# A fp32 two-layer decoder trunk on one NeuronCore: large tiles moved to multiples of 512 bytes, the router's matmul turned round, and result-free matmuls in its waits

## What is computed (the reference, cut)

```
for layer in range(2):
    h = rmsnorm(x, mix_norm[layer]);  z = h @ w_in[layer]            # 1024 x 4392
    q, k, v, qi, ki, wi, u, ga, gp = split(z)
    a = dsa_attention(rope(rmsnorm(q)), rope(rmsnorm(k)), v, rope(qi), rope(ki), wi)   # top 64 keys
    p = pool_mixer(u, w_pool, pool_scale)
    x = x + (sigmoid(ga) * (a @ w_attn_proj) + sigmoid(gp) * (p @ w_pool_proj)) @ w_out
    h2 = rmsnorm(x, ffn_norm[layer])
    layer 0:  x = x + (silu(h2 @ w1) * (h2 @ w3)) @ w2               # 2816 wide
    layer 1:  logits = h2 @ moe_router                               # 8 experts
              top 2 of 8, softmax over the two -> gate
              x = x + sum_e gate[e] * (silu(h2 @ w1[e]) * (h2 @ w3[e])) @ w2[e]   # 3584 wide
```

## Time and profile before

| | |
|---|---|
| three runs | 1588.71 us median (1586.83, 1588.71, 1590.33) |
| the profiled execution | 1589.16 us, its span 1587.3 us |
| PE busy | 1547.0 us, 97% of the span |
| DVE, ACT busy | 1267.5 us, 1052.3 us |
| mean granted TensorE clock | 0.988 of full speed |
| DMA | 445.32 MB, mean 281 GB/s |

### The profile page before, as it was taken

The page is one execution under the profiler, slowest core; times in us unless marked ns, Lnnn a source line. Parts: engine busy times, 40 slices in busy tenths (PEclk is TensorE's granted clock), DMA queues, the critical chain, the costliest instruction groups (busy, mean ns, idle before and its releaser), DMA issues.

```text
span 1587.3 us, 22532 instructions
## 1 busy us (share of the span) xinstructions
PE 1547.0 (97%) x7253; PEld 1270.7 (80%) x7253; DVE 1267.5 (80%) x1329; ACT 1052.3 (66%) x1159; POOL 5.9 (0%) x12
## 2 busy tenths in 40 slices
PE   7999999999999899999999999999999999999997
PEld 6888888788888778878878878877887887887885
DVE  5885655446976579799789789799889979978978
ACT  6565544336464467687687687687778768768766
POOL 0000000000000000000000000000000000000000
PEclk9999999999999789999999999999999999999998
DMA  9543565358543669799899999999989989989985
GB/s 333 160 162 129 186 202 167 106 190 283 167 160 108 234 228 305 262 367 371 290 379 370 313 362 367 330 340 371 373 299 372 373 292 367 369 296 376 372 296 195
DMA packets 329116, 445.32 MB, mean 281 GB/s; under 512 B 14144, under 2 KB 269160, under 8 KB 329080
## 3 DMA queue, kind: packets, MB, share of 16 engines
q1 hardware_dynamic: 328512, 442.71, 81.8%
q0 software_dynamic: 480, 2.13, 0.4%
q10 hardware_dynamic: 88, 0.02, 0.0%
HBM read 443.76 MB, written 1.05 MB: 280 GB/s over the span
## 4 chain that ended last, share of the span: by engine, by line
PE 83%; DMA 4%; issue 4%; DVE 4%; ACT 3%; SPq 1%; DVEq 0%; ACTq 0%
PE bank L746 26%; PE bank L748 25%; PE bank L747 25%; DMA w_raw<-in_moe_w 4%; PE bank L1034 2%; ACT w_hi L448 2%; PE bank L1060 2%; DVE w_lo L1125 1%; DVE hT_lo L1515 1%; SPq L351 1%; PE bank L828 1%; DMA w_raw<-in_w_in 1%; PE bank L772 1%; ACT hT_hi L737 0%; PE bank L812 0%
## 5 line engine op out<-in xcount | busy, mean ns | idle before, releaser
L1125 DVE TENSOR_TENSOR w_lo<-w_raw,w_hi 128x1024 fp32r<-128x1024 f32 (+1 forms) x448 | 780.7, 1755 | 110.8 <-ACT w_hi L448 110.2
L448 ACT ACTIVATE w_hi<-w_raw 128x1024 fp32r<-128x1024 f32 (+1 forms) x448 | 663.8, 1492 | 157.6 <-PE bank L748 143.8
L746 PE MATMUL bank<-w_hi,hT_hi 128*128 128x512 f32 (+1 forms) x1424 | 567.5, 399 | 6.6 <-DVE hT_lo L1515 2.5
L748 PE MATMUL bank<-w_hi,hT_lo 128*128 128x512 f32 (+1 forms) x1424 | 554.9, 390 | 0.0
L747 PE MATMUL bank<-w_lo,hT_hi 128*128 128x512 f32 (+1 forms) x1424 | 553.6, 389 | 0.0
L746 PEld LDWEIGHTS bank<-w_hi,hT_hi 128*128 128x128 f32 x1424 | 268.7, 189 | 62.3 <-issue 6.8
L748 PEld LDWEIGHTS bank<-w_hi,hT_lo 128*128 128x128 f32 x1424 | 268.5, 189 | 56.6
L747 PEld LDWEIGHTS bank<-w_lo,hT_hi 128*128 128x128 f32 x1424 | 269.2, 189 | 50.8
L1120 DVE TENSOR_TENSOR w_lo<-w_raw,w_hi 128x2048 fp32r<-128x2048 f32 (+2 forms) x100 | 201.5, 2019 | 95.6 <-ACT w_hi L442 94.8
L442 ACT ACTIVATE w_hi<-w_raw 128x2048 fp32r<-128x2048 f32 (+2 forms) x100 | 169.6, 1699 | 160.1 <-PE bank L748 158.6
L746 PE MATMUL bank<-w_hi,hiddenM_hi 128*128 128x512 f32 x448 | 178.7, 399 | 1.1
(11 more groups left out here) (230 smaller groups left out, 1022.9 us busy)
## 6 DMA issues: line engine op xcount, KB each, us to landing
w_raw<-in_moe_w SPq DMA_DIRECT2D x672, 512.0 KB
w_raw<-in_w_in SPq DMA_DIRECT2D x64, 512.0 KB
w_raw<-in_dense_w SPq DMA_DIRECT2D x44, 512.0 KB
w_raw<-in_dense_w SPq DMA_DIRECT2D x44, 256.0 KB
w_raw<-in_w_out SPq DMA_DIRECT2D x16, 512.0 KB
w_raw<-in_w_pool_proj SPq DMA_DIRECT2D x8, 512.0 KB
w_raw<-in_w_attn_proj SPq DMA_DIRECT2D x8, 512.0 KB
w_raw<-in_w_in SPq DMA_DIRECT2D x8, 296.0 KB
```

Of the source, the lines that this page charges most:

```text
L448: act.activation(whi[:, m % SLOTS, 0:n], raw8[m % 8][:, 0:n], ACT.Copy).then_inc(s_hi, 1)
L746: pe.matmul(dst, ahi, bhi, start=start, stop=False)
L748: return pe.matmul(dst, alo, bhi, start=False, stop=stop)
L1125: dve.tensor_tensor(wlo[:, m % SLOTS, 0:n], raw8[m % 8][:, 0:n], whi[:, m % SLOTS, 0:n], ALU.subtract).then_inc(s_lo, 1)
```

## The change

Three edits.

1. **Placement.** The small tiles are made first, with two new ones: `sqrt_first` (64 bytes) and `align_512` (192 bytes, never used). The four constants and all small tiles together are then 5120 bytes, ten times 512. So `w_raw`, `w_hi`, `w_lo`, `x_residual`, `hT_hi`, `hT_lo`, and with them `w_raw_7`, `w_raw_456`, `x_rows_hi`, `hiddenM_hi`, the dense layer's `hidden_hi` and the rest of the large ones begin at a multiple of 512. The attention stage's small tiles do not.
2. **Router.** The 8 columns of the router are stationary and 256 columns of hT move: 24 matmuls with an 8 x 256 result. DVE copies this to SBUF (`lgT`), PE transposes it back in two 8-column matmuls. The norm of X comes behind this copy on DVE. ACT makes a first square root (`sq0`) earlier, where the table is loaded; DVE writes only the first token tile's low rows ahead of `select(0)`; the first gather goes token tile by token tile.
3. **Result-free matmuls** of 512 columns (`keep_busy`), whose result nobody reads: 4 ahead of the last transposes, 9 behind the logits' transposes, 3 behind the position matmuls, 6 behind the first gather.

```diff
+        sq0 = sb("sqrt_first", [P, 16])
+        sb("align_512", [P, 48])
+        raw = sb("w_raw", [P, SLOTS, FULL])
...
+        lgT = hsM[0:E, 0, :]
...
@@ ACT, layer()
                 if l == 0:
                     ahead(c + 25)
+                else:
+                    act.activation(sq0[:, 0:1], cst[:, C_ONE:C_ONE + 1], ACT.Sqrt)
                 hT_hi(3 * l + 2, 16 + 8 * l, (2, 3))
                 norm(2 * l + 1)
...
@@ PE
+            def keep_busy(n, b):
+                for _ in range(n):
+                    pe.matmul(bank[b][:], aThi[:, 0, 0:P], aThi[:, 0:2, :], start=True, stop=True)
+
             layer(1, LAYER1, first=lambda: x_T(2, 1))
+            keep_busy(4, 5)
             x_T(3, 1)
...
-                    for t in range(TT):
-                        ins = three(bank[4 + t][:, 0:E], hThi[:, k, t * P:t * P + P], hTlo[:, k, t * P:t * P + P],
-                                    wrhi[:, k, :], wrlo[:, k, :], k == 0, k == KC - 1)
+                    ins = three(bank[4][0:E, 0:S], wrhi[:, k, :], wrlo[:, k, :], hThi[:, k, :], hTlo[:, k, :],
+                                k == 0, k == KC - 1)
             ins.then_inc(s_rt, 1)
+            pe.wait_ge(s_lt, 1)
+            for t in range(TT):
+                ins = pe.transpose(bank[5][:, t * E:t * E + E], lgT[:, t * P:t * P + P], cst[0:E, C_ID:C_ID + E])
+            ins.then_inc(s_rl, 1)
+            keep_busy(9, 0)
             pe.wait_ge(s_mk, 1)
...
+            keep_busy(3, 0)
...
                 pe.wait_ge(s_sel, i + 1)
+                if isinstance(i, int):
+                    for t in range(TT):
+                        pe.wait_ge(s_xrl, t + 1)
...
-            pe.wait_ge(s_xrl, 2)
             gather(0)
+            keep_busy(6, 0)
@@ DVE
                 hT_lo(3 * l + 2, 16 + 8 * l, (2, 3))
-                norm(2 * l + 1)
+                if l == 0:
+                    norm(1)
...
             dve.wait_ge(s_rt, 1)
+            dve.tensor_copy(lgT, bank[4][0:E, 0:S]).then_inc(s_lt, 1)
+            norm(3)
+            dve.wait_ge(s_rl, 1)
             for t in range(TT):
-                ins = dve.tensor_scalar(lg[:, t, :], bank[4 + t][:, 0:E], st[:, 3, t:t + 1], None, ALU.mult)
+                ins = dve.tensor_scalar(lg[:, t, :], bank[5][:, t * E:t * E + E], st[:, 3, t:t + 1], None, ALU.mult)
...
+            rows_lo(0)
             dve.wait_ge(s_pos, 1)
...
             select(0)
+            rows_lo(1)
```

More of the change, by code:

```diff
@@ L96, in sem @@
             return ctx.enter_context(nc.semaphore(name))
[L99 to L104, removed]
         cst = sb("shape_constants", [P, C_END])
@@ L111, in build @@
         wrlo = sb("w_router_lo", [P, KC, E], FR)
+        sq0 = sb("sqrt_first", [P, 16])
+        sb("align_512", [P, 48])
+        raw = sb("w_raw", [P, SLOTS, FULL])
+        whi = sb("w_hi", [P, SLOTS, FULL], FR)
+        wlo = sb("w_lo", [P, SLOTS, FULL], FR)
+        X = sb("x_residual", [P, TT, D])
+        hThi = sb("hT_hi", [P, KC, S], FR)
+        hTlo = sb("hT_lo", [P, KC, S], FR)
         ident = cst[:, C_ID:C_ID + P]
@@ L256, in build @@
         s_rt = sem("router_done")
+        s_lt = sem("router_logitsT_in_sbuf")
+        s_rl = sem("router_logits_done")
         s_gd = sem("gate_diff")
@@ L1024, in _ @@
             pe.matmul(bank[7][:, 0:E], ones, tmp8[:, 1, :], start=False, stop=True).then_inc(s_pos, 1)
+            keep_busy(3, 0)
             def gather(i):
                 pe.wait_ge(s_sel, i + 1)
+                if isinstance(i, int):
+                    for t in range(TT):
+                        pe.wait_ge(s_xrl, t + 1)
+                        for j in range(2):
+                            for q in range(4):
+                                k = 4 * j + q
+                                for x in (xrhi, xrlo):
+                                    ins = pe.matmul(bank[2 + j][:, q * P:q * P + P], x[:, t, k * P:k * P + P],
+                                                    selR[:, t, :], start=(t == 0 and q == 0 and x is xrhi),
+                                                    stop=(t == TT - 1 and x is xrlo), skip_group_check=True)
+                            if t == TT - 1:
+                                ins.then_inc(s_g, 1)
+                    return
                 for j in range(2):
@@ L1445, in _, with rows_lo @@
             dve.nop().then_inc(s_mk, 1)
-            for t in range(TT):
+            def rows_lo(t):
                 dve.wait_ge(s_xr, t + 1)
```

## The result

| | before | after |
|---|---|---|
| median (range), 4 runs each | 1589.32 us (1586.83 to 1590.33) | 1572.82 us (1572.75 to 1573.33) |
| the profiled execution, its span | 1589.16, 1587.3 | 1572.75, 1570.9 |
| PE busy, mean granted clock | 1547.0, 0.988 | 1539.1, 0.991 |
| DMA | 445.32 MB | 445.32 MB |

A forecast was written before the change was run, and what follows sets the result against it. PE, busy 97% of the span, was taken as the bound, so only its waits, half clock or matmul price could move time. Routing and clock 10.1 plus placement 5.4 gave 15.5 us: 1573.2 us, own range 1570 to 1577, 1566 to 1581 at 0.8.

The forecast's parts named there:

- Router, copy, norm, logits, mask, order: Routing's steps up to the gather: logits at 540.55 for 543.86, gather starting at 545.9 for 550.42.
- Sum with the clock full: Routing and first job matmuls at full clock: 7.8 us earlier start plus 2.3 us of faster matmuls, 10.1 us.
- The result-free matmuls: In the routing: all fit into PE's idle time; the nine done by 541.5, or 543.3 at half clock.
- Rival one: Clock falls all the same, once, during the position matmuls: 5.8 + 5.4 = 11.2 us gained, 1577.5 us; chance 0.27.
- the forecast's chain to the first job matmul: Routing through a full-clock gather of 3.52 us: first job matmul near 552.2 for 559.97, 7.8 us earlier.
- Placement on the DMA: Job starts: aligned slots all filled at 385 GB/s, chunks land 0.8 us earlier, 5.4 us in all (bounds 0 and 8.9).
- The bound of some 358 GB/s: Skill page's limit on HBM to SBUF; by it no placement would help and the sum would be 10.1; prediction rejected it.
- PE reads aligned tiles faster: Rival on all 512-column matmuls, some 5,500: 10 ns less each would be 55 us, 1518 us; chance 0.04.
- The sum: Whole kernel: routing with full clock 10.1 plus placement 5.4 gives 15.5 us, for 1573.2 us; forecast's chance 0.47.

The follow-up runs named there:

- no_busy: The changed kernel without its 22 result-free matmuls, the rest the same; median 1573.86 us.
- hold_clock: The changed kernel with 14, 6 and 9 result-free matmuls in place of 9, 3 and 6; median 1569.94 us.
- hold_and_proj: The changed kernel with 14, 6 and 9 result-free matmuls for 9, 3 and 6, and the projections' stationary tiles pT, aT at multiples of 512; median 1567.52 us.
- raw_at_128: The changed kernel with w_raw (slots 0 to 3) alone moved 128 bytes up; median 1578.31 us.
- before_hidden_at_128: The kernel before with 384 bytes of padding ahead of hidden_hi and of hiddenM_hi, putting both at 128 behind a multiple of 512; median 1582.71 us.
- place_only: The kernel before with the changed order of the tiles in SBUF and nothing else of the change; median 1577.56 us.
- route_only: The changed kernel with the large tiles back at their old offsets, 128 and 256 behind multiples of 512; median 1582.27 us.
- raw64_hidden256: The changed kernel with hidden_hi, hiddenM_hi and their lo parts 256 bytes, and w_raw 64 bytes, behind multiples of 512; 1580.44 us, one run.
- changed_again: The changed kernel as it is, run again on the same chip as the clock runs; median 1571.74 us.

## Why the prediction was right, and where it wasn't

- **Router, copy, norm, logits, mask, order: right.** Logits at 540.56 for 540.55, gather at 545.49 for 545.9, with the mixer's end 0.67 earlier. Counted from there the gather is 0.26 late; the norm ran 0.6 long and the way to the mask 0.65 short, both at steps that ran beside POOL's clearing, which the prediction left out. The matmul of 256 columns and 8 stationary ones takes 0.115 us, 0.13 was taken.
- **"Sum with the clock full": wrong in the changed kernel.** The 10.1 us took the gather at 3.52 and the first job matmuls at 0.227; the gather took 6.7 us, and the job's matmuls ran at 0.427 up to 557.4. The result-free matmuls all fitted, but the nine ended at 541.1 and PE then idled 1.70 us before the positions; the idleness was written down, and the forecast put 0.27 on a fall of the clock. Rival one happened as described; its price was 5.8 us for the routing, and 4.4 + 1.1 = 5.5 were measured. In all eight runs with these nine, PE idled 1.70 to 2.55 us there and the clock fell; in no_busy it idled 3.99, and the clock fell 1 us earlier than in the changed kernel; with 14 it idled 0.60, and the clock stayed up (hold_clock, hold_and_proj). hold_clock shows that the forecast's chain to the first job matmul holds when the clock does (19.7 us for 19.4).
- **Placement on the DMA: right.** 385 GB/s in 96 of 107 saturated stretches, 5.1 us of stalls for 5.4, and raw_at_128 takes 5.4 us away when it is undone. The bound of some 358 GB/s that the prediction has from the Trainium skill ("SBUF — State Buffer", section "Summary: rules for kernel authors") doesn't hold in these rows. The distribution was off: job 1's stall hardly shrank (1.44 to 1.36 us in excess, where a fall of 0.8 was forecast), and the others shrank by 0.4 to 1.3. That the sum of seven came out at 5.1 is partly luck.
- **"Nothing in the rows speaks for it" (PE reads aligned tiles faster): wrong, the missed term.** It was priced for 5,500 matmuls (the trace has 6,048) by looking at moving operands alone, which all lay at one offset. The stationary tiles did not, and the trace of before held the difference: 227 ns in the up phases, 232.7 in the jobs' down phases. The prediction took 0.227 from the first rows of job 0 for every matmul. Grouping the distances by the stationary tile's name would have shown 5 ns in some 1,560 matmuls, 7.9 us.
- **The small waits for `w_lo`: not foreseen.** With PE faster in the down phase and DVE not, 15 waits grew by 0.1 us each and gave 1.5 us back. before_hidden_at_128 shows the same growth (4.7 to 6.2) without the rest of the change.
- **The sum** was right since the overstated routing (10.1 for 5.5) and the missed PE term (7.9, less 0.8 and 1.5 given back) cancel. That the range of 1566 to 1581 held around a sum with two such errors is luck.

## What to carry over

Before you trust one number for "a matmul of 512 columns", take its distance by phase and by stationary tile; where it differs at the same clock, compare the byte offsets of the two operands modulo 256. Another order of the tiles and 256 bytes of padding bought 13.0 us here (place_only, by medians; 11.5 by spans), the rewritten routing 8.3 (route_only; 7.1). When a forecast rests on a full clock, look at what PE does in the stretch ahead of each point where it could fall: with PE idle for 1.7 us ahead of the positions it fell, and 11 more result-free matmuls, of which 5 took that idle time to 0.6, held it. Which of the 11 were needed, no run shows.

## What was not expected of the hardware

- The distance of 512-column matmuls depends on the two operands' offsets: 227 to 228 ns when they are equal modulo 256 bytes, 229 to 233 when not (eight pairs of offsets, table above).
- A DMA into SBUF in pieces of 1 KB ran at 385 to 386 GB/s into slots at 0 or 256 modulo 512, and at 348 to 353 into slots at 64 or 128 (before, after, raw_at_128, raw64_hidden256).
- In the changed kernel the length of the half-clock stretch varied between 10.2 and 13.6 us for the same program (changed_again, after), with the jobs' part 1.3 us apart. With the old routing it was 27.3 us in before and 23.9 in place_only and before_hidden_at_128. So a difference of 1 to 2 us around the routing, between two single traces, can be the clock's and not the edit's.
- Small steps of DVE ran long beside POOL's clearing of a tile: 0.66 and 0.82 us for 0.17 (after, before). No run takes the clearing away to test it.
